# The modulation weights of a two-block transformer kernel: folded by VectorE during the front instead of by TensorE during the tiles

## What is computed

```python
mod_all = jnp.einsum('bd,lde->lbe', jax.nn.silu(c), ada_w) + ada_b[:, None]
sh_m, sc_m, gt_m, sh_f, sc_f, gt_f = jnp.split(mod_all[i][:, None, :], 6, axis=-1)
h = modulate(rms_norm(x, norm_g[i, 0]), sh_m, sc_m)
y = stick_breaking_mixer(h, sb_w_qkv[r], sb_w_o[r])
x = x + gt_m * rms_norm(y, norm_g[i, 1])
h = modulate(rms_norm(x, norm_g[i, 2]), sh_f, sc_f)
x = x + gt_f * rms_norm(swiglu_ffn(h, ffn_w_in[i], ffn_w_out[i]), norm_g[i, 3])
```

## Time and profile before

| | |
|---|---|
| median of 3 runs | 2287.61 us |
| the profiled execution | 2291.19 us |
| its span | 2289.4 us |
| busy in the span | PE 81%, weight loads 53%, DVE 56%, ScalarE 39%, POOL 37% |
| granted TensorE clock, mean | 0.872 |
| moved by DMA | 726.17 MB, mean 317 GB/s; gathers 536.90 MB of it |

### The profile page before, as it was taken

One profiled execution on the slowest core, in us unless ns is written; L12 is line 12 of the kernel. 1 busy time (PEld: TensorE's weight loads), 2 busy tenths in 40 slices (PEclk: granted clock), 3 DMA queues, 4 the chain that ended last, 5 costly groups with the idle time before them and its releaser, 6 DMA issues.

```text
span 2289.4 us, 27112 instructions
## 1 busy us (share of the span) xinstructions
PE 1845.8 (81%) x9656; PEld 1203.5 (53%) x9656; DVE 1273.5 (56%) x2864; ACT 893.1 (39%) x2391; POOL 851.1 (37%) x679
## 2 busy tenths in 40 slices
PE   7898898877787868766877675799888779877998
PEld 6784666635454436312344421355455356667997
DVE  4633558877788765556565466665654500433542
ACT  3122344333444433435354545622322420654443
POOL 1300433455655334334333353434333300023654
PEclk9999987867778979877978886999989879998999
DMA  6111999999999999999998899999999944113542
GB/s 252 58 65 37 367 406 398 406 372 407 401 375 414 418 418 417 417 416 416 414 405 343 324 417 419 418 419 418 419 419 418 398 164 129 37 42 143 184 184 111
DMA packets 114583, 726.17 MB, mean 317 GB/s; under 512 B 12945, under 2 KB 12945, under 8 KB 43153
## 3 DMA queue, kind: packets, MB, share of 16 engines
q0 software_dynamic: 73728, 536.90, 57.5%
q1 hardware_dynamic: 40720, 187.54, 21.7%
HBM read 720.20 MB, written 2.10 MB: 316 GB/s over the span
## 4 chain that ended last, share of the span: by engine, by line
PE 49%; DMA 22%; DVE 9%; ACT 8%; issue 6%; POOL 6%; SPq 0%; DVEq 0%; POOLq 0%; ACTq 0%; PEldq 0%
PE ps L895 49%; DMA arena<-in_experts,arena_u 16%; POOL arena L2047 4%; DVE arena L2398 4%; DMA arena<-in_w_ada 3%; DMA gtrow<-in_w_ada 2%; ACT arena L1722 1%; ACT sel L1718 1%; ACT arena L1711 0%; ACT L1772 0%; ACT L1718 0%; POOL arena L2030 0%; POOL r_high L2074 0%; ACT arena L1744 0%; ACT upper L1900 0%
## 5 line engine op out<-in xcount | busy, mean ns | idle before, releaser
L895 PE MATMUL ps<-arena 128*128 128x256 f32 (+4 forms) x6088 | 1294.1, 515 | 276.7 <-ACT arena L1722 236.7
L895 PEld LDWEIGHTS ps<-arena 128*128 128x128 f32 (+2 forms) x6088 | 758.3, 175 | 749.4 <-issue 323.6
L2047 POOL DMA_INDIRECT arena<-in_experts,arena_u x512 | 591.5, 1155 | 906.0 <-PE ps L895 814.1
L2398 DVE CUSTOM_DVE_ANT_0 arena<-arena 128x1024 f32<-128x1024 f32 x512 | 649.6, 1275 | 398.4 <-DMA arena<-in_experts,arena_u 391.7
L1718 ACT ACTIVATE sel<-sel 128x1 f32<-128x1 f32 x512 | 102.2, 200 | 661.0 <-DVE sel L2398 657.5
L2074 POOL TENSOR_TENSOR r_low<-middle,r_low 128x1024 fp32r<-128x1024 f32 x48 | 122.2, 2551 | 257.6 <-ACT r_low L1876 257.6
L1722 ACT ACTIVATE arena<-arena,sel 128x32 f32<-128x32 f32 x512 | 164.5, 321 | 16.8
L895 PE MATMUL ps<-r_low 128*128 128x256 f32 (+1 forms) x1104 | 141.7, 292 | 11.6 <-POOL r_low L2074 5.9
L895 PEld LDWEIGHTS ps<-r_low 128*128 128x128 f32 x1104 | 138.2, 195 | 15.0 <-POOL r_low L2074 6.7
L895 PE MATMUL ps<-arena,consts 128*32 128x512 f32 (+5 forms) x656 | 88.4, 443 | 52.9 <-POOL arena L2030 36.9
L1711 ACT ACTIVATE arena<-consts,arena 128x32 f32<-128x32 f32 x512 | 120.7, 307 | 0.0
(11 more groups left out here) (244 smaller groups left out, 1550.7 us busy)
## 6 DMA issues: line engine op xcount, KB each, us to landing
arena<-in_w_front SPq DMA_DIRECT2D x88, 512.0 KB, 3.6
middle<-in_w_late SPq DMA_DIRECT2D x18, 2048.0 KB, 7.9
arena<-in_w_qkv SPq DMA_DIRECT2D x48, 512.0 KB, 4.3
arena<-in_w_late SPq DMA_DIRECT2D x22, 1024.0 KB, 13.8
gtrow<-in_w_ada SPq DMA_DIRECT2D x32, 512.0 KB
arena<-in_w_late SPq DMA_DIRECT2D x30, 512.0 KB
arena<-in_experts,arena_u POOLq DMA_INDIRECT x512
arena<-in_w_ada SPq DMA_DIRECT2D x16, 512.0 KB
```

Source lines behind the costliest of these rows:

```text
L895: return nc.tensor.matmul(out_, lhsT, rhs, start=start, stop=stop_, skip_group_check=skip)
L2047: nc.gpsimd.indirect_dma_start(ring[n % RING], None, a["experts"], bass.IndirectOffsetOnAxis(ap=idxq[:, i % 4, k:k + 1], axis=0),).then_in ...
L2398: nc.vector.tensor_tensor_reduce(r[:, 0:D], r[:, 0:D], xrep[k % 4], 1.0, 0.0, ALU.mult, ALU.add, dots[:, n % 8:n % 8 + 1]).then_inc(s["dot ...
```

## The change

Three parts.

- The weights are laid out as 48 loads of 128x1024 (each row block of `ada_w` times one of six parts) and read into four slots at 144 to 160 KB of the arena during the front of half 0. A new stage `ad` stands 48 times in the list of half 0: one behind each `u` of the levels (12), two behind each `kc` (4), two behind each `pm` (8), three behind each of `wo` 0 to 3 (12), one behind `os`, `ob`, `om`, three behind `wo` 4 and two behind `wo` 5 to 7.
- In `ad` DVE multiplies a load with one number for each partition and adds it to one of three accumulators of 128x2048. For every sixteenth and the load behind it (six in all) it is a `tensor_scalar`, for the others a `scalar_tensor_tensor`. SP refills the slot.
- PE only adds over partitions: stage `ar` (8 matmuls with ones, two banks) and `aw` (8 matmuls that turn rows into columns) before and behind `tr1`, with ScalarE's copies; and four matmuls with ones for the gates (`gp`), where 64 with the vector stood. The matmuls and the waits of `modulation` in the tiles are gone; `gp` takes 24 steps of the list instead of 36.

```diff
@@ front_plan
+    ada = iter(range(ADA_RUNS))
+    def run(n):
+        for _ in range(n if h == 0 else 0):
+            add("ad", next(ada))
...
                 add("u", (c, lv), 2)
+                run(1)
...
             add("kc", c)
+            run(2)
...
             add("pm", g)
+            run(2)
...
             add("wo", k)
+            run(3)
     add("os", 0, 1)
+    run(1)
     add("ob", 0, 1)
+    run(1)
     add("om", 0, 1)
+    run(1)
     for k in range(4 if h == 0 else 0, OUT_UNITS):
         add("wo", k, 2)
+        run(3 if k == 4 else 2)
     add("xa", 0, 2)
+    if h == 0:
+        add("ar")
     add("n1", 0, 1)
     add("tr1", 0, 3)
+    if h == 0:
+        add("aw")
...
-        for k in range(4 * N_GATE):
-            add("gp", k, 2)
-            if k % 4 == 1 and k > 4:
-                add("gs", k // 4 - 1)
-        add("gs", N_GATE - 1, 4)
+        for m in range(N_GATE):
+            add("gp", m, 4)
+            add("gs", m, 2)
@@ SyncE
+            def ada_load(k):
+                if k >= ADA_RUNS:
                     return
+                if k >= ADA_SLOTS:
+                    sp.wait_ge(s["mfree"], k - ADA_SLOTS + 1)
+                sp.dma_start(ada_unit[k % ADA_SLOTS], a["w_ada"][k]).then_inc(a_unit[k % ADA_SLOTS], 16)
...
-            pair(0)
-            pair(1)
+            for k in range(ADA_SLOTS):
+                ada_load(k)
...
-                done = mod_pairs(at, done)
...
+                elif stage == "ad":
+                    ada_load(arg + ADA_SLOTS)
@@ TensorE
                 elif stage == "xr0":
+                    pe.wait_ge(s["mod"], 4)
...
+                elif stage == "ar":
+                    pe.wait_ge(s["mfree"], ADA_RUNS)
+                    pe.wait_ge(s["os"], 2)
+                    for r in range(2):
+                        for q in range(4):
+                            ins = mm(ps[32 * q:32 * q + 32, 7 * r, :], const(C_ONES)[:, 0:32], ada_acc[1 + r][:, q * HALF:(q + 1) * HALF])
+                        ins.then_inc(s["gfree"], 1)
+                elif stage == "aw":
+                    for r in range(2):
+                        pe.wait_ge(s["mod"], r + 1)
+                        for j in range(4):
+                            ins = mm(ps[:, 7 * r, j * P:(j + 1) * P], mod_rows[:, r, j * P:(j + 1) * P], ident)
+                        ins.then_inc(s["gfree"], 1)
                 elif stage == "gp":
...
+                    mm(ps[:, m, :], const(C_ONES), ada_acc[0][:, m * HALF:(m + 1) * HALF]).then_inc(s["gfree"], 1)
...
-                if k is not None and mod_load(k) == n:
-                    modulation(k)
-                    k = next(mods, None)
@@ ScalarE
                     sc.wait_ge(s["sc"], Q_UNITS * h + j + 1)
+                    if h == 0 and j == 0:
+                        sc.wait_ge(s["mfree"], ADA_RUNS)
...
+                elif stage == "ar":
+                    for r in range(2):
+                        sc.wait_ge(s["gfree"], r + 1)
+                        nc.scalar.activation(mod_rows[:, r, :], ps[:, 7 * r, :], ACT.Copy, scale=0.5).then_inc(s["mod"], 1)
...
-                if n % TOPK == 12 and i < N_MODC:
-                    sc.wait_ge(s["mfree"], 4 * i + 4)
-                    nc.scalar.activation(flat(modc)[:, 4 * i:4 * i + 4], ps[:, 5, 64 + 4 * i:68 + 4 * i], ACT.Copy, scale=0.5).then_inc(s["mod"], 1)
@@ VectorE
+                elif stage == "ad":
+                    k, kd = arg, arg % 16 // 2
+                    dst = ada_acc[k // 16][:, k % 2 * D:(k % 2 + 1) * D]
+                    if k == 0:
+                        ve.wait_ge(s["cs"], 1)
+                    if k == 16:
+                        ve.wait_ge(s["o"], 2)
+                    ve.wait_ge(a_unit[k % ADA_SLOTS], 16 * (k // ADA_SLOTS + 1))
+                    if kd == 0:
+                        ts(dst, ada_unit[k % ADA_SLOTS], ccol[:, 0:1], None, ALU.mult).then_inc(s["mfree"], 1)
+                    else:
+                        ve.wait_ge(s["mfree"], k - 1)
+                        stt(dst, ada_unit[k % ADA_SLOTS], ccol[:, kd:kd + 1], dst, ALU.mult, ALU.add).then_inc(s["mfree"], 1)
```

More of the change, by code:

```diff
@@ L422, in block_kernel @@
         narrow = [region(48 + 4 * n, D) for n in range(NARROW)]
-        mpair = gtrow[:, :, :].rearrange("p s (k n) -> p s k n", k=2)
-        gpair = [region3(48 + 4 * n, 2, HALF) for n in range(2)]
+        ada_unit = [region(144 + 4 * n, D) for n in range(ADA_SLOTS)]
+        ada_acc = [gtrow[:, :, :].rearrange("p k n -> p (k n)"), region(80, 2 * D), region(88, 2 * D)]
+        mod_rows = region3(60, 2, HALF)
         gacc = gtrow[:, :, :].rearrange("p k (b n) -> p (k b) n", b=2)
-        rows = region3(60, 2, HALF)
+        rows = region3(48, 2, HALF)
         hT = region3(64, KD, SH)
@@ L558, in h_turn @@
             n = h_slot(m)
-            before = sum(unit_slot(k)[0] == WIDE + n for k in range(QUERY0, 2 * FRONT)) if n < NARROW else MODS // 2
+            before = sum(unit_slot(k)[0] == WIDE + n for k in range(QUERY0, 2 * FRONT)) if n < NARROW else ADA_RUNS // ADA_SLOTS
             return before + sum(h_slot(k) == n for k in range(m + 1))
         def f_turn(j):
-            before = 2 * N_GATE if j % F_SLOTS < 2 else 0
+            before = ADA_RUNS // ADA_SLOTS if j % F_SLOTS < 2 else 0
             return before + j // F_SLOTS + 1
@@ L714, in block_kernel @@
         w_unit = [sem(f"w_unit{n}") for n in range(WIDE + NARROW)]
-        m_pair = [sem(f"m_pair{n}") for n in range(2)]
-        g_pair = [sem(f"g_pair{n}") for n in range(2)]
+        a_unit = [sem(f"a_unit{n}") for n in range(ADA_SLOTS)]
         w_late = [sem(f"w_late{n}") for n in range(2)]
         gathered = [sem(f"gathered{n}") for n in range(RING)]
-        h_unit = w_unit[WIDE:] + m_pair
-        f_unit = g_pair + [sem("f_unit")]
+        h_unit = w_unit[WIDE:] + a_unit[0:2]
+        f_unit = a_unit[2:4] + [sem("f_unit")]
         block = ctx.enter_context(nc.Block())
@@ L782, in front_unit @@
                     unit(k + NARROW)
-            done = 2
             for at, h, stage, arg in STAGES:
-                done = mod_pairs(at, done)
                 if stage == "p":
@@ L1223, in rotate @@
                 mm(ps[64:P, 7, :], ident[:, 0:64], rotated(t), False, True, True).then_inc(s["swapped"], 1)
-            def modulation(k):
-                n, kd = k // 4, k % 4 * 2
-                pe.wait_ge(s["cs"], 1)
-                pe.wait_ge(m_pair[k % 2], 16 * (k // 2 + 1))
-                if kd == 0:
-                    pe.wait_ge(s["idx"], n + 2)
-                for lane in range(2):
-                    for j in range(4):
-                        ins = mm(ps[:, 5, 64 + 4 * n + j:65 + 4 * n + j], mpair[:, k % 2, lane, j * P:(j + 1) * P],
-                                 ccol[:, kd + lane:kd + lane + 1], kd + lane + j == 0, kd + lane == KD - 1, True)
-                ins.then_inc(s["mfree"], 1)
             def tile_transposes(t):
@@ L1373, in qkv_unit @@
                 ins.then_inc(s["used"], 1)
-            mods = iter(range(MODS))
-            k = next(mods)
             for n in range(LOADS):
@@ L2046, in load @@
                     pl.wait_ge(s["slot_done"], n - RING + 1)
+                elif n >= RING - 2:
+                    pl.wait_ge(s["gfree"], 2)
                 nc.gpsimd.indirect_dma_start(
@@ L2534, in laid_out @@
         "sub_keys": g["sub_keys"][0].reshape(2 * PH, NK, P).transpose(2, 0, 1),
-        "w_front": np.concatenate(front), "w_late": np.concatenate(late), "w_qkv": np.concatenate([columns(w_qkv[:, :2 * D]), w_values]), "w_ada": chunks(adaw),
+        "w_front": np.concatenate(front), "w_late": np.concatenate(late), "w_qkv": np.concatenate([columns(w_qkv[:, :2 * D]), w_values]), "w_ada": adaw.reshape(KD, P, 6, D).transpose(2, 0, 1, 3)[[4, 5, 0, 1, 2, 3]].reshape(3, 2, KD, P, D).transpose(0, 2, 1, 3, 4).reshape(ADA_RUNS, P, D),
         "experts": np.concatenate([g["expert_down"][0], g["expert_up"][0]], axis=1),
```

58 lines of the change are left out of this document (16 added, 42 removed).

## The result

The change makes the kernel faster: 2263.23 us in the median (2257.26 to 2268.51) against 2287.67 for the kernel before (2286.96 to 2289.76), a ratio of 0.9897 with a 95% interval of 0.9875 to 0.9919. The forecast was 2249.5 with a range of 2232 to 2277. The profiled execution took 2263.32 us with a span of 2261.5 at a mean granted clock of 0.868, so the span is 27.9 us shorter than before.

A forecast was written before the change was run, and what follows sets the result against it. It took DMA to bound most of the gather, with DMA, DVE and PE near balance from 250 to 655 us. 2291.2 - 20.2 - 35 + 17.1 = 2253.1, less 3.6 is 2249.5 us; range 2232 to 2277.

The forecast's parts named there:

- Gate stretch: Gate weights' stretch in the gather: removing 8.39 MB of loads at 416 GB/s saves 20.2 us, taken whole.
- Heads 0 to 7: First heads of the gather: fewer load bytes save 35 us, DVE limiting heads 2 and 3; removed PE matmuls counted nothing.
- Rival B: Heads 0 to 7: the compute chain, not DMA, sets the pace; only 12 us gained there, 2272.5 us; chance 0.13.
- Rival C: Whole gather: ring-slot turns set the pace and bytes cost nothing; only the front's cost remains, 2304.7 us; chance 0.05.
- A: Whole kernel: all removed bytes count and the front costs 12 to 13 us, 2238 us; chance 0.06 with anything beyond.
- E: Before the gather: the added loads slip back into it, so the change does not do what it says; no chance given.
- Front: Before the gather begins: the added loads and DVE additions cost 17.1 us, bounds 12 and 27.
- six levels: Levels in the front: additions between chunk 0 and chunk 1 delay DVE's answers to PE, together 3.4 us.
- `pm` to `om`, with 20 additions: Front: 20 additions at `pm` and `wo` 0 to 3 make `wo` 4 start 9.0 us late.
- So the stream is even with DVE: Front loads: a four-slot turn, landing in 3.4 to 3.6 us, gives 1.25 to 1.30 us per load, matching DVE.
- Rival D: Front: additions starve for loads at 3.3 us each, costing 59 us more, 2308 us; chance 0.03.
- forecast clock dip: `wo` in the front: PE's lower clock after some 8 us idle costs 2 us, bounds 0 and 3.5.

The follow-up runs named there:

- e10: The kernel after run again unaltered, beside other kernels on the same chip; 2261.56 us, ratio 0.9913.
- e1: The kernel before with 46 of its 48 `w_ada` loads left out and PE's matmuls kept; 2259.95 us, ratio 0.9889.
- e12: The kernel after with the 512 one-column tile matmuls put back on constants, without loads; 2277.05 us, ratio 0.9962.
- e2: The kernel before with all loads but 25 of each head's 32 tile modulation matmuls taken out; 2274.8 us, ratio 0.9951.
- e4: The kernel after with full-size additions but only the first four loads read; 2250.97 us, ratio 0.9858.
- e5: The kernel after with six slots for the `w_ada` loads instead of four; 2253.14 us, ratio 0.9854.
- e6: The kernel after with additions spread, nine between levels and `pm`, none at `os`, `ob`, `om`, second accumulator moved; 2250.52 us, ratio 0.9837.
- e3: The kernel after with all loads, but the 42 `scalar_tensor_tensor` only eight columns wide; 2250.18 us, ratio 0.985.
- e7: e6 with each level's two additions together behind chunk 1 and ScalarE's `ar` copies behind `n1`; 2249.82 us, ratio 0.9842.
- e11: e7 run again, beside the kernel after on the same chip; 2246.57 us, ratio 0.9826.

## Why the prediction held, and where its steps did not

The time fell inside the range, and inside the forecast's own 2238 to 2264, close to its end: the forecast was 13.7 us too low. Step by step:

**Gate stretch, 20.2 us.** Right, within 2 us. Heads 14 to 17 are 20.4 us shorter in the kernel after, 18.7 in its repeat e10, and 17.9 in e1, where only the loads went. The reason held too: DVE waits for gathers there before and after.

**Heads 0 to 7, 35 us by bytes, PE at nothing.** This step failed in mechanism and, with 26.1 us, in size. For pairs 1 and 2 it was right: 11.5 and 6.1 us against 9.5 and 6.2, DVE's limit in heads 2 and 3 included. For pairs 3 and 4 it gave 19 and 8.5 came. The sentence that failed is that these pairs "are not held by" DVE and therefore by bytes. With 72 to 74 us of DVE and 72 to 74 of PE in 91 and 102 us no single engine was near its limit, and still DMA was not the pace: taking its bytes away gained nothing (e1), and putting PE's matmuls back cost 14.6 us there (e12 against after). That it was the chain gather, dot, weight, sums, release fits this, though no run took another link out of it; in the trace of before, the chain of work that ended last holds 37.1% PE and 7.7% gathers from 461 to 654 us. Rows that pointed to it were used in the prediction: DMA at 390 and 391 GB/s in these pairs against 411 and 401 in the first two, and POOL waiting 189.7 us for PE. A share of 0.97 was read as full, though the rate was 5% lower. "Counted at nothing" for 78 us of PE work was the other error: e2 puts 25 of 32 matmuls at 13.2 us, e12 all of them at 18.4. The bytes were put at 35 us and are worth 8.5 alone (e1). That the sum came within 9 us is luck: 26 us too much for the bytes and 18 too little for PE.

**Rival B** (12 us in heads 0 to 7) was right on heads 4 to 7, where DMA is not the pace, and wrong on the size, as it too gave PE's work no value. DMA's share of 0.88 in heads 4 and 5, with the heads only 3.7 us shorter, speaks for it there; the sign that the prediction gave for it, heads 2 and 3 as long as before, did not come (6.1 us shorter). **Rival C** is excluded by heads 14 to 17, 20 us shorter; **A** by heads 4 to 7 and by the front; **E** by DMA's strip, which is filled ahead of the gather, and by the first gather's delay.

**Front, 17.1 us with bounds of 12 and 27.** 23.2 came. Against the terms, each as a difference of distances in the two timelines:

| piece | forecast | measured |
|---|---|---|
| six levels | 3.4 | 2.5 |
| behind the levels to `pm`: clock dip | 0 | 1.6 |
| `pm` to `om`, with 20 additions | 9.0 | 14.1 |
| `om` to `n1` on DVE: clock dip, `ar` | 4.4 | 3.7 |
| `n1` to the first gather: `aw` | 0.3 | 1.3 |
| sum | 17.1 | 23.2 |

The levels, timeline of the kernel after: the addition stands in the gap that the earlier trace rows showed. From the start of L2244 to that of L2243 it is 1.79 us, where before, with the 0.50 us of idle time in it, it was 1.18: 0.61 late, forecast 0.78. Four times 0.61 and what the first level adds are the 2.5 us.

```profile
110.02 0.68 DVE L2244 TENSOR_TENSOR arena<-arena,ps 128x512 f32<-128x512 f32 x1
110.62 1.28 DVE L2327 SCALAR_TENSOR_TENSOR gtrow<-arena,ccol,gtrow 128x1024 f32<-128x1024 f32 x1
111.81 0.68 DVE L2243 TENSOR_TENSOR arena<-arena,ps 128x512 f32<-128x512 f32 x1
```

Behind the levels PE has the same 56 small matmuls in front of `pm`, in the kernel before (first row) and after:

```profile
157.13 8.16 PE L895 MATMUL ps<-arena 128*128 128x128 f32 x56
...
160.72 9.78 PE L888 MATMUL ps<-arena 128*128 128x128 f32 x56
```

They took 1.6 us longer, at a granted clock of 0.90 from 153 to 170 us against 1.00 from 149 to 166 before: for part of it TensorE was at 1.2 GHz. The prediction had no term for it. All six profiles with an addition between chunk 0 and chunk 1 have it (after, e4, e5, e6, e10, e12: `pm` is 4.1 us late in each). In e3, whose additions are tiny, and in e7 and e11, where both stand behind chunk 1, the grant falls to the lower level only later, and `pm` is 0.1 to 0.5 us late.

The additions ahead of `os` (L2279 is its reciprocal), DVE of the kernel after:

```profile
170.53 1.42 DVE L2324 TENSOR_SCALAR arena<-arena,ccol 128x1024 f32<-128x1024 f32 x2 [0.66 <-PE ps L888]
171.86 2.48 DVE L2327 SCALAR_TENSOR_TENSOR arena<-arena,ccol 128x1024 f32<-128x1024 f32 x2
...
177.34 3.85 DVE L2327 SCALAR_TENSOR_TENSOR arena<-arena,ccol 128x1024 f32<-128x1024 f32 x3 [1.34 <-DMA arena<-in_w_ada]
...
199.94 1.28 DVE L2327 SCALAR_TENSOR_TENSOR arena<-arena,ccol 128x1024 f32<-128x1024 f32 x1 [1.09 <-DMA arena<-in_w_ada]
201.14 0.20 DVE L2279 RECIPROCAL arena<-arena 128x8 f32<-128x8 f32 x1
```

From 170.5 to 201.1 they took 30.6 us; the forecast had 24.6 and 0.7 for `zg`. Of this, 6.7 us are waits for loads, nine of them of 0.3 to 1.3 us, which the forecast had at nothing. Without waits it would be less than forecast, 22.4 us in e4; 1.06 us of the difference is that all 12 additions at `wo` 0 to 3 were priced at 1.28 us, though two of them are `tensor_scalar`. "So the stream is even with DVE" was the step that failed: the turn of a slot was put at 1.25 to 1.30 us for each load with a landing of 3.4 to 3.6 us, and in the stream itself a landing took 5.4 us (e3; some 5.2 for these 20 loads in e10, the same kernel as after). With six slots the waits are gone (e5). Rival D named this and put it at a time of its own (3.3 us for each addition); the truth was between, at 1.5 us. PE then shows the idle time in front of `ob`, 9.25 us where some 8 were forecast:

```profile
176.66 16.21 PE L888 MATMUL ps<-arena 128*128 128x512 f32 x32 [0.77 <-ACT arena L1648]
202.12 3.43 PE L888 MATMUL ps<-arena,consts 128*128 128x512 f32 x4 [9.25 <-DVE arena L2282]
207.97 15.67 PE L888 MATMUL ps<-arena 128*128 128x512 f32 x32 [2.43 <-DVE arena L2289]
```

The last row against the earlier trace rows is the forecast clock dip: the same 32 matmuls took 15.67 us instead of 13.97, 1.7 us where 2 were forecast. The first row shows another, ahead of that idle time: `wo` 0 to 3 took 16.21 us at a granted clock of 0.86, against 13.97 at 1.00 before. It is hidden behind DVE's additions.

**Two rules of the Trainium skill.** Ports: in the kernel after an addition behind chunk 1 takes 1.48 us (first row) instead of 1.28 where POOL's masks run beside them (second row), with idle time behind them, so it costs nothing there, as forecast.

```profile
113.01 1.48 DVE L2327 SCALAR_TENSOR_TENSOR gtrow<-arena,ccol,gtrow 128x1024 f32<-128x1024 f32 x1
...
112.14 1.27 POOL L1977 TENSOR_TENSOR arena<-arena 128x512 f32<-128x512 f32 x1 [3.20 <-PE ps L888]
```

In e7, with two additions in one place, the pair took 4.30 us instead of 2.5 once, beside two such instructions of POOL.

```profile
104.33 4.30 DVE L2327 SCALAR_TENSOR_TENSOR gtrow<-arena,ccol,gtrow 128x1024 f32<-128x1024 f32 x2
...
104.07 1.27 POOL L1977 TENSOR_TENSOR arena<-arena 128x512 f32<-128x512 f32 x1 [3.20 <-PE ps L888]
105.77 1.77 POOL L1977 TENSOR_TENSOR arena<-arena 128x512 f32<-128x512 f32 x1 [0.44 <-PE ps L888]
```

The Trainium skill ("SBUF — State Buffer", Terms) says that VectorE and GpSimd arbitrate for a shared port pair and the loser blocks. These rows agree in direction, the size is 0.2 us in the one place and 0.9 for each addition in the other. The 358 GB/s that the Trainium skill gives on the same page ("A bandwidth-pool intuition that's wrong") for HBM to one core is again below what was moved, 418 GB/s in heads 0 and 1.

**The sum.** The terms miss by 8.9 us (heads 0 to 7), 6.1 (front) and 1.1 (the first "identity minus" later, by PE's first blocks at the lower clock, last section), against 0.2 gained beyond the forecast in the gate stretch and 5.7 in stretches that were forecast unchanged: 38.1 us forecast for the profiled execution, 27.9 measured. The rest of the 13.7 is that the profiled execution before lay 3.6 us above its median and that of the kernel after at its median.

## What to carry to other kernels

A DMA share near 1 in a stretch does not say that bytes are its pace: compare the rate with that of the stretch where DMA surely is (390 against 416 GB/s here), and price both the bytes and the matmuls that go with them, since near balance each is worth part of its time and both together more than either. Work moved onto an in-order engine costs by where it stands, not by how much there is: the same 48 additions cost 23 us or 4 to 7 us. A stream through few slots is priced with the landing that a load has within the stream (5.4 us here), not with that of a load by itself (3.4 to 3.6); here two slots more took the waits away.
